# A two-block transformer kernel on one core: where rounds of weight sums are placed, when the input sums begin, and where some stores and a store wait are issued

## The reference, cut to what matters

```python
x = x + swa_sink_mixer(rms_norm(x, swa_norm), swa_w_in, ...)      # first block
#   q, k, v, gate = split(h @ w_in); windowed attention with sinks; (o * silu(gate)) @ w_out
h = concatenate([meta_tokens, x])                                  # second block: 16 more rows
hn = _rmsnorm(h, attn_norm_w)
a_q, a_k, a_v, a_g, b_cq, b_ckv, b_kr, b_g = split(hn @ w_in)
oA = _diff_attention(qA, kA, vA, lam, slopes)                      # 8 heads, two softmaxes each
qB = _rmsnorm(b_cq) @ w_uq;  kvB = _rmsnorm(b_ckv) @ w_ukv
oB = _mla_attention(q_nope, rope(q_pe), k_nope, rope(b_kr), vB)    # 8 heads
h = h + concatenate([oA * silu(a_g), oB * silu(b_g)]) @ w_out
y = _rmsnorm(h, final_norm_w)[:, 16:528]
```

## Time and profile before

| | |
|---|---|
| time, median of 3 runs | 1662.81 us (1662.02 to 1663.41) |
| the profiled execution | 1661.9 us; its span 1660.1 us |
| PE busy | 1628.6 us, 98% of the span |
| DVE, ACT, POOL busy | 852.2, 818.2, 671.3 us |
| mean granted clock of PE | 0.994 |
| DMA | 281 MB, mean 169 GB/s |
| queue of SyncE (q1), of POOL (q0), of ACT (q10) | 29.8%, 24.3%, 7.1% of 16 DMA engines |

### The profile page before, as it was taken

How to read it: one execution, slowest core, us unless ns; L and a number is a source line. 1 busy time by engine, 2 the same in 40 slices (tenths; PEclk the granted TensorE clock), 3 DMA queues, 4 the chain that set the end, 5 groups by cost and what they waited for, 6 DMA issues and landing times.

```text
span 1660.1 us, 22638 instructions
## 1 busy us (share of the span) xinstructions
PE 1628.6 (98%) x8343; PEld 1350.4 (81%) x8343; DVE 852.2 (51%) x1934; ACT 818.2 (49%) x1759; POOL 671.3 (40%) x569
## 2 busy tenths in 40 slices
PE   9999999999999999999999999999999999999998
PEld 7788898888888888888788877787877777888886
DVE  3356656663123766259545440423335455767574
ACT  3356666765334454443445455444456565444551
POOL 4463423334665602566110024544444434665022
PEclk9999999999999999999999999999999999999999
DMA  6585535245878877988787558856474512324772
GB/s 227 153 211 124 128 89 128 80 124 128 185 175 195 222 228 218 281 224 196 216 196 229 158 180 257 276 127 192 104 213 105 152 59 77 102 96 126 242 246 101
DMA packets 139595, 281.13 MB, mean 169 GB/s; under 512 B 11051, under 2 KB 19052, under 8 KB 139324
## 3 DMA queue, kind: packets, MB, share of 16 engines
q1 hardware_dynamic: 86012, 160.29, 29.8%
q0 software_dynamic: 31664, 81.70, 24.3%
q10 hardware_dynamic: 21808, 37.68, 7.1%
HBM read 254.68 MB, written 92.06 MB: 209 GB/s over the span
## 4 chain that ended last, share of the span: by engine, by line
PE 83%; DVE 6%; DMA 4%; ACT 2%; issue 2%; POOL 2%; ACTq 0%; DVEq 0%; POOLq 0%
PE acc L684 15%; PE acc L686 15%; PE acc L685 15%; PE turn L781 3%; PE acc L825 2%; PE acc L824 2%; PE acc L826 2%; PE turn L1120 2%; PE turn L824 2%; PE turn L825 2%; PE turn L826 2%; PE sc L826 2%; PE sc L825 2%; PE sc L824 2%; PE turn L706 2%
## 5 line engine op out<-in xcount | busy, mean ns | idle before, releaser
L1807 POOL TENSOR_TENSOR w_lo<-w_raw,w_hi 128x512 fp32r<-128x512 f32 x341 | 507.4, 1506 | 783.4 <-ACT w_hi L1236 772.4
L1236 ACT ACTIVATE w_hi<-w_raw 128x512 fp32r<-128x512 f32 x565 | 352.6, 628 | 438.2 <-PE acc L686 215.6
L684 PE MATMUL acc<-w_hi,setA_hi 128*128 128x512 f32 (+1 forms) x1088 | 445.9, 410 | 7.1 <-POOL w_lo L1807 4.1
L686 PE MATMUL acc<-w_hi,setA_lo 128*128 128x512 f32 (+1 forms) x1088 | 422.9, 389 | 0.0
L685 PE MATMUL acc<-w_lo,setA_hi 128*128 128x512 f32 (+1 forms) x1088 | 421.6, 387 | 0.0
L684 PEld LDWEIGHTS acc<-w_hi,setA_hi 128*128 128x128 f32 x1088 | 206.0, 189 | 47.1 <-issue 11.1
L686 PEld LDWEIGHTS acc<-w_hi,setA_lo 128*128 128x128 f32 x1088 | 205.1, 189 | 42.7
L685 PEld LDWEIGHTS acc<-w_lo,setA_hi 128*128 128x128 f32 x1088 | 206.6, 190 | 29.8
L2183 DVE TENSOR_TENSOR w_lo<-w_raw,w_hi 128x512 fp32r<-128x512 f32 x224 | 155.5, 700 | 143.8 <-ACT w_hi L1236 143.5
L1321 ACT ACTIVATE p_w<-sm,negm 128x256 f32<-128x256 f32 (+1 forms) x128 | 60.6, 474 | 57.2 <-DVE sink_d L2071 57.2
L1644 ACT ACTIVATE p<-sm,negm 128x144 f32<-128x144 f32 (+3 forms) x96 | 54.3, 566 | 56.7 <-DVE negm L2489 38.8
(11 more groups left out here) (519 smaller groups left out, 3124.9 us busy)
## 6 DMA issues: line engine op xcount, KB each, us to landing
w_raw<-in_swa_w_in SPq DMA_DIRECT2D x35, 1024.0 KB, 7.7
w_raw<-in_w_in SPq DMA_DIRECT2D x32, 1024.0 KB, 6.6
w_raw<-sum_out SPq DMA_DIRECT2D x64, 256.0 KB, 4.2
sum_k<-in_w_in POOLq DMA_DIRECT2D x24, 512.0 KB, 7.8
sum_out<-in_swa_w_out POOLq DMA_DIRECT2D x24, 512.0 KB, 7.6
sum_v<-in_w_in POOLq DMA_DIRECT2D x24, 512.0 KB, 8.0
w_raw<-in_w_in SPq DMA_DIRECT2D x48, 256.0 KB, 3.0
sum_out<-in_w_out POOLq DMA_DIRECT2D x24, 512.0 KB, 7.8
```

The costliest lines, as they stand in the source:

```text
L684: mm(acc[t][:, 0:cols], hi[:, kc, rows], wh, start=(k == 0), stop=False)
L686: last = mm(acc[t][:, 0:cols], lo[:, kc, rows], wh, start=False, stop=(k == K - 1))
L1236: nc.scalar.activation(w_at(f)[0], raw_of(f), ACT.Copy).then_inc(done, 1)
L1807: nc.gpsimd.tensor_tensor(lo, raw_of(f), hi.bitcast(F32), ALU.subtract).then_inc(s_lo, 1)
```

## The change

It moves work and leaves the amount of it as it is: no DMA and no operation is added or dropped.

- Rounds: chunk 1 has none; k0 is in chunk 2, out1 0 in 3 and 4 as before, k1 in 5, out1 1 to 3 in 6 to 8, k2 in 9, k3 in pair out1 (from tile 12), v0 in chunk 12 as before, none in 13, v1 in 14, v2 and v3 in pair k (from tiles 0 and 26), out2 0 and 1 in pair v (likewise), none from chunk 19 to 29, out2 2 and 3 in chunks 30 and 31. In pairs a helper paces a round's steps, one every one and a half tiles.
- Input sums: DVE makes part 0 ahead of the residual add in chunk 13, part 1 in the same chunk before `ss_1`, parts 2 and 3 in chunk 14; ACT's splits stand at k of 2 in chunk 13 and 1, 8 and 12 in chunk 14.
- Stores behind pair v: the two `store_meta` at k of 0 of chunk 20, `left` at k of 2 of chunk 20, the turn of `kpe` and its evacuation at k of 1 in place of 0.
- POOL's wait for the previous body's store is at Q of 36 inside the body.

```diff
-for slot, of in enumerate((("k", 0), ("k", 1), ("out1", 0), ("k", 2), ("out1", 1), ("out1", 2), ("out1", 3), ("k", 3),
+for slot, of in enumerate((("k", 0), ("out1", 0), ("k", 1), ("out1", 1), ("out1", 2), ("out1", 3), ("k", 2), ("k", 3),
@@ PE, chunks 19 to 21
-                    if c == 1 and k == 0:
+                    if c == 1 and k == 1:
@@ ACT, chunk 13
-                if k == 13:
+                if k == 2:
                     act.wait_ge(s_used, B[13] + 4)
                     split_s("x", 0)
@@ ACT, chunk 14: split_s("x", 1), ("x", 2), ("x", 3)
-                if k == 3:   ...   if k == 9:   ...   if k == 13:
+                if k == 1:   ...   if k == 8:   ...   if k == 12:
@@ ACT, chunks 19 to 21
-                    if c == 0 and k == 3:
-                        store_half(12, left, 2 * CW, s_st)
+                    if c == 1 and k == 0:
                         for part in range(2):
                             store_meta(2, kv_d, (2 + part) * CW, part)
-                    if c == 1 and k == 0:
+                    if c == 1 and k == 1:
                         act.wait_ge(s_kpe_ps, 2)
...
-                    if c == 1 and 1 <= k < 3:
-                        scale_part("v", 3, k - 1)
+                    if c == 1 and k == 2:
+                        store_half(12, left, 2 * CW, s_st)
+                    if c == 1 and k >= 2:
+                        scale_part("v", 3, k - 2)
@@ POOL
+            def paced_sums(c, i, during, first):
+                for k in range(KC):
+                    pool.wait_ge(s_used, B[during] + first + 3 * k // 2 + 4)
+                    block_sums(c, i, k)
+
+            paced_sums("k", 3, "out1", 12)
...
-                    block_sums("v", c - 12, k)
+                    if c == 14:
+                        block_sums("v", 1, k)
...
-            for k in range(KC):
-                pool.wait_ge(s_used, B["k"] + 3 * k + 4)
-                block_sums("v", 3, k)
+            paced_sums("v", 2, "k", 0)
+            paced_sums("v", 3, "k", 26)
             root(r_cq[:], ss_cq[:], NT, ROOT_CQ)
+            paced_sums("out2", 0, "v", 0)
+            paced_sums("out2", 1, "v", 26)
...
+                    if Q == 36 and stored:
+                        pool.wait_ge(s_st, stored * 16)
...
-            pool.wait_ge(s_st, 4 * 16)
-            attend_loads(MLA, 1, 26, (DIFF, 0))
-            pool.wait_ge(s_st, 5 * 16)
-            attend_loads(DIFF, 0, 28, (DIFF, 1))
+            attend_loads(MLA, 1, 26, (DIFF, 0), 4)
+            attend_loads(DIFF, 0, 28, (DIFF, 1), 5)
...
                     split_lo(30 + c, k)
+                    if c < 2:
+                        block_sums("out2", 2 + c, k)
@@ DVE, chunks 13 and 14
+            dve.wait_ge(s_turn_lo, 44 + EARLY)
+            dve.wait_ge(s_x1d, 96)
+            x1_sums(0)
             dve.wait_ge(s_evac, 4 * E[12] + 8)
             dve.wait_ge(s_xin, 32)
             V.tensor_tensor(stage[:], stage[:], x_in[:], ALU.add).then_inc(s_x1, 1)
...
-            dve.wait_ge(s_turn_lo, 48 + EARLY)
-            dve.wait_ge(s_x1d, 96)
-            x1_sums(0)
+            split_s_lo("x", 0)
+            x1_sums(1)
             (the reduction of ss_1)
-            split_s_lo("x", 0)
-            x1_sums(1)
+            split_s_lo("x", 1)
+            dve.wait_ge(s_turn_lo, 48 + EARLY)
+            x1_sums(2)
```

More of the change, by code:

```diff
@@ L1524, in _ @@
                                   a["diff_lambda"].rearrange("a d -> (a d)").partition_broadcast(P)).then_inc(s_lam, 16)
-                if k == 3:
+                if k == 1:
                     split_s("x", 1)
@@ L1534, in _ @@
                     nc.scalar.activation(lam_s[:], lam_s[:], ACT.Exp).then_inc(s_lam, 1)
-                if k == 9:
+                if k == 8:
                     split_s("x", 2)
-                if k == 13:
+                if k == 12:
                     split_s("x", 3)
@@ L1578, in _ @@
                         turn_hi(52 + k - 1, k - 1, ckvT_hi[:, k - 1], gain_ckv[:, k - 1:k])
-                    if c == 0 and k < 2:
-                        scale_part("v", 0, k)
-                    elif c == 0:
-                        scale_part("v", 1, k - 2)
-                    if c == 0 and k == 3:
-                        store_half(12, left, 2 * CW, s_st)
+                    if c == 0:
+                        scale_part("v", k // 2, k % 2)
+                    if c == 1 and k == 0:
                         for part in range(2):
                             store_meta(2, kv_d, (2 + part) * CW, part)
-                    if c == 1 and k == 0:
+                    if c == 1 and k == 1:
                         act.wait_ge(s_kpe_ps, 2)
@@ L1854, in _ @@
                 split_lo(1, k)
-                block_sums("k", 0, k)
                 if k == 8:
@@ L1863, in _ @@
                         if g in (0, 3):
-                            block_sums("k", 2 if g else 1, H // 2)
+                            block_sums("k", 1 if g else 0, H // 2)
                         if g == 1 and H >= 8:
@@ L1874, in _ @@
                 split_lo(9, k)
-                block_sums("k", 3, k)
+                block_sums("k", 2, k)
+            def paced_sums(c, i, during, first):
[3 more added lines that the diff above has]
+            paced_sums("k", 3, "out1", 12)
             for f in range(B[12], B[12] + AHEAD):
@@ L1938, in _, with attend_loads @@
             turned_by = {A: turn_uses(A) for A in (MLA, DIFF)}
-            def attend_loads(A, i, c0, then):
+            def attend_loads(A, i, c0, then, stored=0):
                 for Q in range(4 * KC):
@@ L1944, in attend_loads @@
                         split_lo(c0 + i, Q // 4)
-                        if A.mla or i == 0:
-                            block_sums("out2", 1 + i if A.mla else 3, Q // 4)
                     if A.mla and i == 0 and Q == 11:
@@ L1963, in _ @@
                 split_lo(19, k)
-                block_sums("out2", 0, k)
                 if k == 17:
@@ L2395, in _ @@
             last.then_inc(s_lam, 1)
-            split_s_lo("x", 1)
-            x1_sums(2)
+            split_s_lo("x", 2)
+            x1_sums(3)
             dve.wait_ge(s_kpeT, 1)
@@ L2401, in _ @@
                                        gain_ckv[:, f:f + 1], ckvmT[:, f, 0:META].bitcast(F32), ALU.mult, ALU.subtract).then_inc(s_ckvm, 1)
-            split_s_lo("x", 2)
-            x1_sums(3)
             dve.wait_ge(s_lam, 18)
```

## The result

The changed kernel takes 1651.3 us (median of 8 runs, 1647.05 to 1654.17), the kernel before 1662.1 us beside it (8 runs, 1655.83 to 1663.41). The ratio is 0.9942, with a 95% interval of 0.9922 to 0.9962 (all ratios here are against the kernel before, run beside the variant): some 10 us less where 23 were forecast, outside the range given. The profiled execution took 1647.05 us (span 1645.2); forecast were 1638.7 for it.

What follows compares the result with a forecast made beforehand. PE was taken as the bound, busy 1628.6 of 1660.1 us, leaving its stalls and half-clock stretches to win. The terms summed to -23.2 us: 1661.9 to 1638.7 profiled, 1639.6 as a median, range 1636 to 1646.5.

Steps and rivals of the forecast that it cites:

- G: Rounds added in pairs out1, k, v and chunks 30, 31 cost 0; bounds 0 to +6 for out1, 0 to +1 for the chunks.
- B: Chunks 13 to 14: no round in 13, input sums before the residual add; both waits and half clock go, -6.7 us.
- A: Chunk 1: without a round, the wait of 0.97 us on a slow load goes, -0.95 us.
- Rival 1: Chunk 13: input sums delay the residual add; PE waits at worst 2.8 us plus 1.4 for the clock, 1643.8; 12%.
- C: Chunk 14 to pair k: earlier sums 2 to 4 end the wait on DVE's w_lo and its half clock, -4.2 us.
- D: Chunk 19 to 20: stores moved so ACT's evacuation starts sooner; a wait of 0.6 stays, -3.7 us.
- E: Chunk 22 to 23: no rounds under chunks 19 to 25, so kv_d<-right lands sooner, -5.1 us with the half clock.
- F: Attention: no rounds and POOL's store wait at Q of 36 remove nat_q and kd_lo waits, -2.5 of 2.7 us.
- rival 3: Pair out1 runs short of tiles for a moment, +3 and +1.4 us, 1644.0; 8%.
- rival 2: A part of C, D or E stays because the next thing is late, 2 to 5 us each, 1642 to 1645; 20%.
- rival 5: The rounds were not the cause, only D's order counts; 14.3 us of B, E and F stay, 1653.9; 4%.
- rival 4: Slower: five rounds in three pairs take the tile loads' bandwidth, 30 us lost at 90 GB/s, 1669.8; 5%.

Runs made afterwards that it cites:

- the last version: sums_in_gaps with the last DMA of round out2 1 issued behind POOL's eighth split from chunk 19 on, not ahead of the first; 1637.8 us, ratio 0.9863.
- the rounds alone: Kernel before with only the changed places of the rounds; input sums, ACT's splits, stores and POOL's store wait as before; 1648.2 us, ratio 0.9940.
- k3_early: Changed kernel with round k3 begun at tile 0 of pair out1 in place of tile 12; 1645.8 us, ratio 0.9921.
- the rest alone: Changed kernel with all rounds back where the kernel before had them; input sums, stores and POOL's store wait as changed; 1655.6 us, ratio 0.9984.
- sums_in_gaps: Changed kernel with two part-0 additions in DVE's gaps ending chunk 12, k rounds as before, out2 2 and 3 in chunks 28, 29; 1640.8 us, repeated 1639.2.
- bodies_wait_first: Changed kernel with out2 2 and 3 in chunks 28, 29 and POOL's store wait of chunk 28 again ahead of its first split; 1650.5 us, ratio 0.9939.
- kback_sums_bodies: Changed kernel with k rounds and DVE's input-sum order as before, out2 2 and 3 in chunks 28, 29, ACT's last splits earlier; 1639.2 us, ratio 0.9875.
- copies_by_act: Changed kernel with the four copies opening round out2 3 in chunk 31 issued by ACT's queue in place of POOL's; 1644.7 us, ratio 0.9916.

## Why the prediction was wrong, step by step

Two steps failed: the rounds' new places were priced at nothing (G), and the residual add behind the input sums was taken as on time (B).

- **A** (-0.95): chunk 1 -1.2. Right; with the round back in it, in the last version, it took 46.25 again, with a wait of 1.0.
- **B** (-6.7): the part on the rounds was right, chunks 13 and 14 together fall by 7.1 with the rounds alone (86.16 to 79.08). Rival 1, given 12%, came as written: the add late, PE waiting at the turn, 2.3 us of a priced 2.8. Half clock did not follow here, but did in k3_early, where the wait was 2.6 and chunk 13 took 39.47: 4.4 more than the 35.08 without it, against a price of 4.2. So chunks 13 and 14 fall by 4.6 and not by 6.7: this step was 2.1 short, by a rival that it named.
- **C** (-4.2): pair k -4.4. The size was right and the credit not: the rounds alone bring 3.3. The last 1.1, of which 0.8 is a wait, came only with DVE's order. The rest alone shows 4.4, but its chunk 14 is 4.9 longer, which gives DVE time, so it does not say what the order is worth alone.
- **D** (-3.7): chunk 20 -3.7, with the residual wait of 0.4 us (0.6 was priced). Right, and due to the stores alone.
- **E** (-5.1): chunk 23 -4.9; the rounds alone give all of it, and `kv_d<-right` lands in 6.8 us, in under the 10 named as the sign. Right.
- **F** (-2.5): chunks 26 to 28 -3.3, a little more than forecast, and for a reason half misread. It laid both waits on `nat_q` to the opening waits, but the first (1.06 us, at 1064.25 before) is in chunk 26, which has none: there the round alone cost. The rounds alone give all of the 3.2, the rest alone 0.8. Only in chunks 27 and 28 do wait and round cost together and not singly.
- **G** (0, bounds 0 to +6 and 0 to +1): +9.6. **This is the main step that failed**: "I take 0", and the range counted hardly any of the bounds. Three places. Pair out1 itself: +1.1 (nothing to +3.2 in the six executions with this round at this place), tiles landing in up to 11.6 us (613.19 to 624.82) against the "about 5" in the sum of slack; PE waited 0.64 us, so rival 3 came in small. Chunk 12: +4.8, where the term looked inside the pair alone; the round ended late, and the first load of chunk 12, behind tile loads that had become late beside the round, took 10.5 us. How much of the 4.8 this is, is known only roughly: chunk 12 without a late round took 50.6 to 52.5. Chunks 31 and 32: +2.7 (to +5.3), where "built as chunks 6 to 8" left out the root and the sub-scaling on DVE: the bracket named the root, and the sum then took nothing for it. Chunk 2, where k0 stands in place of k1 and for which no term stood, adds +1.0 (0.8 wait on `stage`).

The total: of the 23.2 us forecast, G took back 9.6 and B 2.1, which leaves 11.5; A, C, D, E and F together gave 1.0 more than forecast, chunk 0 gave 2.0 and small ones 0.4: 14.9, from 1661.9 to 1647.05. With G's places mended, 1637.8 is reached against the 1638.7 forecast. That this is so near is in part luck: A's 0.95 is given up again and chunk 12 costs 1.0, while chunk 0, which no edit touches, gives 1.8 and F 0.7 more than forecast.

What the list of signs got right: evacuation 13 without a wait on the root, no stretch at half clock from 700 to 1060 in the changed kernel's own execution, `kv_d<-right` in 6.8 us, DMA share of pair out1 at 0.96. What it missed: a PE wait over 1.2 us at 719, and a gap of 0.64 in pair out1; and it watched the pairs, not the chunks behind them. The chances do not add up either: the forecast and rivals 1, 2, 3 and 5 have 95%, which leaves 5% to rival 4, and not 94% and 6%. Rival 4 (bandwidth) did not come in its strong form: the pairs k and v ran at a share of 0.97 each with no wait in PE. Windows of after, out1, k, v:

```profile
572.55:649.83 77.28, 76.64 (x337) 62.92 (x336) 42.60 (x62) 39.29 (x68) 6.75 (x9) 1.00 0.96 273
788.10:879.60 91.50, 91.50 (x402) 73.45 (x401) 49.04 (x79) 41.53 (x67) 14.38 (x18) 1.00 0.97 252
879.60:972.90 93.30, 93.30 (x418) 74.98 (x417) 48.32 (x74) 41.12 (x66) 14.33 (x18) 1.00 0.97 270
```

Open: why executions of one program still lie 2 to 10 us apart (chunk 0 took 56.9 or 58.9 us, chunk 31 47.8 or 51.4), what in chunk 12 keeps it between 50.6 and 52.5 with no late round, and how much of the smaller differences a second profile of each kernel would change: only the changed kernel and sums_in_gaps were profiled twice.

## What to carry to other kernels

Background DMAs moved into a stretch with slack are priced at its end, not inside it: ask when the last of a chain of dependent transfers lands, which first load or first split of the next stretch it meets, and what is queued behind its wait. An engine that catches up after a wait takes another one's turns; in two of the three bodies looked at, a wait or extra work was free and both together were not; in the third the extra work alone cost. A term set at nothing with a bound of +6 should still have widened the range; here it came to 9.6.

## What of the hardware was not expected

An operation of DVE with two inputs in SBUF (128x512) took 0.68 us undisturbed and 5.86 us (the second of the four scalings at 1430.23) while POOL did splits and DMA issues in turn without a gap: longer than one split of 1.31 us. Between plain splits back to back a like operation took 1.78 us in the rest alone (at 761.60), and so did each of the four scalings with ACT issuing. The Trainium skill, SBUF — State Buffer, Who interferes with whom, says that two inputs of DVE contend with a GpSimd instruction that reads SBUF; these 1.78 us agree. That an issue between two splits keeps DVE out as well is what the exchange with ACT's queue points to (9.87 to 6.88 us for four); it was not tried by itself. It is not needed for a long one: beside three plain splits in a row DVE operations of this kind took 4.64 us before, and 4.71 and 4.96 with ACT issuing. Why DVE and POOL take turns in one place, and DVE stands out a whole run in another, is open.

The length of a stall did not decide alone whether half clock followed. It did behind 3.2 us in chunk 12, 2.6 us at the turn in chunk 13 (k3_early), 2.0 us in chunk 28 (bodies_wait_first) and 1.4 us at pair k (kback_sums_bodies); it did not behind 2.7 us in chunk 12 (copies_by_act), nor behind 2.3 us at the turn and 2.0 us in chunk 31 of the changed kernel.
